# The triangle inverse of the RWKV-7 chunks: left columns only, and the two heads as tiles of 64 rows by 64 columns

## The chip, the cores and the metric

The kernel runs on one core of a Trainium2 chip. The metric is the device time of one execution in microseconds (us), taken as the median of three runs. The profile and the trace are of one further execution of the same program.

## The reference, cut to what matters

The program computes two blocks in a row over 512 tokens (528 in the second, with 16 meta tokens) of width 1024. The change touches only the RWKV-7 layer of the second block. Its recurrence, for each of 32 heads of width 64, is

```python
def step(S, inp):
    r_t, w_t, k_t, v_t, a_t, b_t = inp
    sa = jnp.einsum('bhij,bhj->bhi', S, a_t)
    S = S * w_t[:, :, None, :] + sa[..., None] * b_t[:, :, None, :] + v_t[..., None] * k_t[:, :, None, :]
    return S, jnp.einsum('bhij,bhj->bhi', S, r_t)
```

The kernel does it in chunks of 64 tokens. Inside a chunk the steps hang on each other through a triangular 64x64 matrix, `(I - M)` with `M` strictly triangular, and the kernel needs its inverse for each of the 9 chunks of each head.

## The kernel before

The 32 heads are done as 16 pairs; a tile has head 0 of the pair on partitions 0 to 63 and head 1 on partitions 64 to 127 (`own[0]`, `own[1]`). `all_passes` runs 18 passes, written out for each engine. Pass `i` works on three pairs at once: part A makes the projections of pair `i` (`a_products`, L1348 and L1361), part B the Gram matrices and the inverse of pair `i-1`, part Cs the scan over the chunks of pair `i-2`. Passes 1 to 15 have A and B, pass 16 has B and Cs but no A.

The order on TensorE (PE) is written by hand. First come the nine steps of the scan, each waiting for VectorE (DVE) or ScalarE (ACT); then, in part B, the transposes (L1490), the Gram products (L1499) and the five levels of the inverse. Between the pieces `fill(k)` puts k steps of `a_products`, of four trace records each, or in pass 16 steps of `wo_unit` (L159 to L161 on whole 128x128 weights). `FILL_X` and `FILL_T` put two steps behind each product of a level:

```python
FILL_TURN, FILL_GRAM, FILL_FIRST, FILL_END = 4, 8, 5, 4
FILL_X, FILL_T = (2, 2, 2, 2, 2), (2, 2, 2, 2, 2)
```

The inverse doubles its block size from level to level. `t_m` holds the inverse so far, `t_t` its transpose. A level is: X = M·T (L1510) into PSUM banks 2 and 3; DVE multiplies it with the mask of the level into `x_m` (L1835); the second product with `t_t` (L1526, at level 5 L1528) goes to banks 4 and 5; DVE adds it to `t_m` (L1841) and transposes that (L1844), or at level 5 adds it into `tb` (L1847). The 9 chunks go in two parts of 4 and 5 chunks (`PARTS`), with a semaphore for each.

For each chunk and head there is one call of the matmul with fp32 operands, and each call stands as two records (and two weight loads) in the trace. The contraction runs over all 128 rows: `mb` and `x_m` hold one head and zeros where the other head is, so `mb` is laid out as [128, 9, 128] and `x_m` as [128, 9, 2, 64]. The output of head h has 64 columns of the array. The trace calls such a tile 128*64. `late_pads` writes the zeros once; `x_m` gets its zeros anew from the mask `lv_pad`, which is padded in the same way.

Of the kernel before, what the change touches and what calls it, by code (L numbers as in the profile page):

```python
# [12 lines left out]
ALU = mybir.AluOpType  # L13
# [5 lines left out]
P = 128  # L19
# [51 lines left out]
def program(nc, io, out):  # L71
    with ExitStack() as base:
# [1172 lines left out]
        tb = put("tb", [P, NC_, P])  # L1245
        rb = put("rb", [P, NC_, P])
        t_m = put("t_m", [P, NC_, C])
        x_m = put("x_m", [P, NC_, 2, C])
        t_t = put("t_t", [P, NC_, C])
        bk_rows = put("bk_rows", [P, NC_, P])  # L1250

# [5 lines left out]
        cent, pair_mask = raw[1][:, KD * P:KD * P + P], raw[1][:, KD * P + P:KD * P + P + C]  # L1257
        z_hl = put("z_hl", [P, 2, T2], F32R)
        assert put.end <= LV_PAD, put.end
        lv_pad = region(LV_PAD)("lv_pad", [P, 5, 2, C])  # L1260
        assert LV_PAD + 2.5 <= 147.75

        sb_a, sb_c = xT[:, 0:2, :], xT[:, 2:4, :]
# [43 lines left out]

        def chunks(buf):
            return buf[:].rearrange("p (a b) -> p a b", b=C)

        def halves_of(buf, at=PAD):
            return buf[:, at:at + T2].rearrange("p (a b) -> p a b", a=2)
# [63 lines left out]
        def wo_unit(pe, n):  # L1376

            u = U_WO + n
            pe.wait_ge(split_ready, u + 1)
            if n < 14 or n > 15:  # L1380
                m, half = WO_TILES[n]
                pairs = range(KD * half, (KD if half == 0 else PAIRS - 2 if m < EARLY else PAIRS))
                todo = [(k - KD * half, k, WO_BANKS[m], k == 0, k == (PAIRS - 3 if m < EARLY else PAIRS - 1)) for k in pairs]
                if half == 0:
                    if m == 0:
                        pe.wait_ge(a_ev, 12 * PAIRS)
                        pe.wait_ge(s_z, 48)
                    elif m == 1:
                        pe.wait_ge(wo_ev, 2)
                    elif m == 2:  # L1390
                        pe.wait_ge(tl_ev, 4 * PAIRS)
                        pe.wait_ge(gn_ln, PAIRS - 1)
                    elif m == 4:
                        pe.wait_ge(wo_ev, 4)
                    elif m > 4:
                        pe.wait_ge(m_out, {5: 1, 6: 2, 7: 5}[m])
            else:
                tiles = (0, 1) if n == 14 else (2,)
                pe.wait_ge(wo_ev, 6)
                pe.wait_ge(m_out, 3 if n == 14 else 4)  # L1400
                todo = [(len(tiles) * j + q, PAIRS - 2 + j, LEFT_BANKS[m], j == 0, j == 1) for q, m in enumerate(tiles) for j in range(2)]
            for q, (b, k, banks, start, stop) in enumerate(todo):
                if k >= READY:
                    pe.wait_ge(z_pool, 4 * (k + 1))
                for h in range(2):
                    at = h * (T2 // 2)
                    x = z_hi[:, k, at:at + T2 // 2], z_lo[:, k, at:at + T2 // 2]
                    mm = product(ps[:, banks[h], 0:T2 // 2], block_of(u % 2, b), x, start, stop)
                    if h == 1 and q == len(todo) - 1:
                        mm.then_inc(unit_done, 1)  # L1410
                    yield

        def pass_pe(pe, i, A, B, Cs):
# [17 lines left out]
            for n in range(NC_):  # L1431
                if Cs:
# [11 lines left out]
                    if n == 8:  # L1444
                        pe.wait_ge(yy_ev, 3 * c + 1)
                    if n == 0:
                        pe.wait_ge(tl_ev, 4 * c + 4)
                    for h in range(2):
                        nc.tensor.matmul(y_at(n)[own[h], :], uv[:, n, h, :], rb[:, n, own[h]], start=True, stop=False)
                    if 0 < n < NC_ - 1:  # L1450
# [24 lines left out]
            if B:  # L1475
# [27 lines left out]
                for lv in range(1, 6):  # L1503
                    for p, (c0, m) in enumerate(PARTS):
                        if lv == 1:
                            pe.wait_ge(mb_ev, 4 * b + (2 * p + 2))
                        pe.wait_ge(tm_ev if lv == 1 else tadd_ev, 2 * b + (p + 1) if lv == 1 else 8 * b + (2 * (lv - 2) + p + 1))
                        for x in range(m):
                            for h in range(2):
                                mm = nc.tensor.matmul(ps[own[h], 2 + p, x * C:x * C + C], mb[:, c0 + x, own[h]], t_m[:, c0 + x, :],  # L1510
                                                      start=True, stop=True)
                        mm.then_inc(x_mm, 1)
                        if lv == 1 and p == 0:
                            fill(FILL_FIRST)
                    fill(FILL_X[lv - 1])
                    for p, (c0, m) in enumerate(PARTS):
                        pe.wait_ge(x_ev, 10 * b + (2 * (lv - 1) + p + 1))
                        if lv == 1:
                            pe.wait_ge(t0_ev, 6 * b + (2, 6)[p])
                        else:  # L1520
                            pe.wait_ge(tb_ev, 8 * b + (2 * (lv - 2) + p + 1))
                        for x in range(m):
                            for h in range(2):
                                dst = ps[own[h], 4 + p, x * C:x * C + C]
                                if lv < 5:
                                    mm = nc.tensor.matmul(dst, t_t[:, c0 + x, :], x_m[:, c0 + x, h, :], start=True, stop=True)  # L1526
                                else:
                                    mm = nc.tensor.matmul(dst, x_m[:, c0 + x, h, :], t_t[:, c0 + x, :], start=True, stop=True)  # L1528
                        mm.then_inc(tt_mm, 1)
                    fill(FILL_T[lv - 1])  # L1530
                    if lv == 3 and A:
# [222 lines left out]
            ge(dve, fa, 14 * i + (FA["e_ex"] - 14))  # L1754
            nc.vector.tensor_tensor_scan(lsum[:], restart[:], ws_b[:], 0.0, ALU.mult, ALU.add).then_inc(scanned, 1)

        EARLY_PADS, MIDDLE_PADS, PADS = 6, 14, 20

        def early_pads(dve):
            for h in range(2):  # L1760
# [15 lines left out]
        def late_pads(dve):  # L1776
            dve.wait_ge(mx_done, 4 * KD)
            for buf in (mb, tb, rb):
                nc.vector.memset(buf[:], 0.0).then_inc(pads, 1)
            nc.vector.memset(lv_pad[:], 0.0).then_inc(pads, 1)  # L1780
            dve.wait_ge(pads, PADS - 2)
            for h in range(2):
                nc.vector.tensor_copy(lv_pad[own[h], :, h, :], lv_mask[own[h], 1:6, :]).then_inc(pads, 1)

        def pass_dve(dve, i, A, B, Cs):
            b, c = i - 1, i - 2
# [40 lines left out]
                nc.vector.transpose(t_m[:, c0:c0 + m, :], t_t[:, c0:c0 + m, :]).then_inc(tm_ev, 1)  # L1827

            def part_of(bank, m):
                return ps[:, bank, 0:m * C].rearrange("p (a b) -> p a b", b=C)  # L1830

            def level(lv):
                for p, (c0, m) in enumerate(PARTS):
                    dve.wait_ge(x_mm, 10 * b + (2 * (lv - 1) + p + 1))
                    nc.vector.tensor_tensor(x_m[:, c0:c0 + m, :, :], part_of(2 + p, m).unsqueeze(2).to_broadcast([P, m, 2, C]),  # L1835
                                            lv_pad[:, lv - 1, :, :].unsqueeze(1).to_broadcast([P, m, 2, C]),
                                            ALU.mult).then_inc(x_ev, 1)
                for p, (c0, m) in enumerate(PARTS):
                    dve.wait_ge(tt_mm, 10 * b + (2 * (lv - 1) + p + 1))
                    if lv < 5:  # L1840
                        nc.vector.tensor_tensor(t_m[:, c0:c0 + m, :], part_of(4 + p, m), t_m[:, c0:c0 + m, :],  # L1841
                                                ALU.add).then_inc(tadd_ev, 1)
                        dve.wait_ge(tadd_ev, 8 * b + (2 * (lv - 1) + p + 1))
                        nc.vector.transpose(t_t[:, c0:c0 + m, :], t_m[:, c0:c0 + m, :]).then_inc(tb_ev, 1)  # L1844
                    else:
                        for h in range(2):
                            nc.vector.tensor_tensor(tb[own[h], c0:c0 + m, own[h]], part_of(4 + p, m)[own[h], :, :],  # L1847
                                                    t_t[own[h], c0:c0 + m, :], ALU.add).then_inc(tl_ev, 1)
            if B:
                dve.wait_ge(g_mm, 3 * b + 1)  # L1850
                gram_out(0)
# [28 lines left out]
        def pass_pool(pool, i, A, B, Cs):  # L1880
# [10 lines left out]
            if B:  # L1891

                if Cs:
                    pool.wait_ge(tl_ev, 4 * c + 4)
                held(pool)
                nc.gpsimd.tensor_copy(t_t[:], ident_2[:].unsqueeze(1).to_broadcast([P, NC_, C])).then_inc(eye_done, 1)
                pool.wait_ge(eye_done, b + 1)
# [956 lines left out]
```

## Time and profile before

| | us |
|---|---|
| median of 3 runs | 2376.39 (2374.34 to 2379.22) |
| the profiled execution | 2373.65 |
| span of its trace | 2371.9 |
| PE busy | 2295.2 (97% of the span) |
| DVE busy | 1235.5 (52%) |
| POOL busy | 1142.6 (48%) |
| ACT busy | 851.7 (36%) |

The span is what the trace covers; the profiled execution's own time has 1.75 us around it. "Busy" is time in which at least one instruction of the engine was in flight. PE stands for the matmuls and PEld for the weight loads, which run beside matmuls.

### The profile page before, as it was taken

How to read it: one execution, taken by the hardware profiler on the slowest of the kernel's cores; microseconds unless marked ns; L12 is line 12 of the kernel's file. 1: busy time of each engine (PE TensorE's matmuls, PEld its weight loads, DVE VectorE, ACT ScalarE, POOL GpSimd, SP SyncE). 2: the span in 40 equal slices, each digit the busy share in tenths (PEclk: the TensorE clock that was granted, in tenths of full speed). 3: DMA queues.
4: the chain of work that ended last, by engine and by line, in shares of the span. 5: the costliest groups of instructions: out<-in, count | busy, mean ns of one | idle time of the engine just before them, and what ended most of it. 6: DMA issues, size and time to landing. Idle time of an engine off the chain costs nothing.

```text
span 2371.9 us, 51852 instructions
## 1 busy us (share of the span) xinstructions
PE 2295.2 (97%) x22065; PEld 1789.5 (75%) x22065; DVE 1235.5 (52%) x2284; ACT 851.7 (36%) x1762; POOL 1142.6 (48%) x771
## 2 busy tenths in 40 slices
PE   8999999999999999999999999999899999999898
PEld 7788787788887677777777777777688887777776
DVE  4353278577804555555555555555421566556511
ACT  4122112233302445555555555555221343343300
POOL 4555566866763434443444333344356344344245
PEclk9999999999999999999999999999799999999899
DMA  3333233233322312222222222221523322121212
GB/s 111 89 80 78 83 90 88 80 98 98 108 98 64 92 57 72 69 66 66 66 66 70 72 66 66 66 66 56 183 68 114 105 70 61 41 61 52 83 58 93
DMA packets 263757, 188.07 MB, mean 79 GB/s; under 512 B 18267, under 2 KB 242393, under 8 KB 263145
## 3 DMA queue, kind: packets, MB, share of 16 engines
q1 hardware_dynamic: 263529, 184.76, 26.0%
q8 instruction: 176, 2.88, 0.5%
q14 instruction: 52, 0.43, 0.1%
HBM read 162.69 MB, written 22.04 MB: 78 GB/s over the span
## 4 chain that ended last, share of the span: by engine, by line
PE 61%; DVE 2%; POOL 1%; DMA 1%; issue 1%; ACT 0%; SPq 0%; POOLq 0%; DVEq 0%
PE ps L1348 18%; PE ps L159 7%; PE ps L160 6%; PE ps L161 6%; PE ps L1510 3%; PE ps L1526 3%; PE ps L1552 2%; PE ps L2388 2%; PE ps L1466 1%; PE ps L1499 1%; PE ps L1438 1%; PE ps L1361 1%; PE ps L221 1%; DMA z_lo<-z_kept 1%; PE ps L2374 1%; PE ps L1483 1%
## 5 line engine op out<-in xcount | busy, mean ns | idle before, releaser
L150 POOL TENSOR_TENSOR w_lo<-raw,w_hi 128x1024 fp32r<-128x1024 f32 (+1 forms) x196 | 494.8, 2524 | 16.4
L147 POOL TENSOR_SCALAR w_hi<-raw 128x1024 fp32r<-128x1024 f32 (+1 forms) x196 | 217.1, 1108 | 559.1 <-PE ps L161 542.1
L159 PE MATMUL ps<-h_hi,w_hi 128*128 128x512 f32 x616 | 244.2, 396 | 5.7 <-POOL w_lo L150 4.6
L161 PE MATMUL ps<-h_hi,w_lo 128*128 128x512 f32 x616 | 240.9, 391 | 0.0
L160 PE MATMUL ps<-h_lo,w_hi 128*128 128x512 f32 x616 | 240.4, 390 | 0.0
L1885 POOL TENSOR_TENSOR kp<-k_b,kp 128x528 f32<-128x528 f32 x16 | 29.6, 1847 | 362.0 <-ACT kp L1647 362.0
L1348 PE MATMUL ps<-mixed_r,raw 128*64 128x264 f32 x1024 | 154.4, 391 | 2.3 <-ACT g_b L1589 2.3
L159 PEld LDWEIGHTS ps<-h_hi,w_hi 128*128 128x128 f32 x616 | 116.3, 189 | 31.9 <-POOL w_lo L150 7.2
L1348 PE MATMUL ps<-mixed_k,raw 128*64 128x264 f32 x1024 | 138.3, 389 | 0.0
L161 PEld LDWEIGHTS ps<-h_hi,w_lo 128*128 128x128 f32 x616 | 115.9, 188 | 24.8
L160 PEld LDWEIGHTS ps<-h_lo,w_hi 128*128 128x128 f32 x616 | 116.2, 189 | 23.2
L1835 DVE TENSOR_TENSOR x_m<-ps,lv_pad 128x512 f32<-128x512 f32 (+1 forms) x160 | 115.1, 753 | 33.2 <-PE ps L1510 29.2
L1348 PE MATMUL ps<-mixed_g,raw 128*64 128x264 f32 x1024 | 132.2, 386 | 0.0
L1348 PE MATMUL ps<-mixed_v,raw 128*64 128x264 f32 x1024 | 129.6, 386 | 0.0
L1078 DVE SCALAR_TENSOR_TENSOR up_c<-up_raw,params,up_c 128x512 f32<-128x512 f32 x88 | 111.3, 1266 | 31.8 <-ACT up_c L830 30.2
L1510 PEld LDWEIGHTS ps<-t_m,mb 128*64 128x64 f32 x2880 | 99.9, 138 | 15.0
L1510 PE MATMUL ps<-t_m,mb 128*64 128x64 f32 x2880 | 100.4, 222 | 0.0
L2475 ACT ACTIVATE xT<-ps,nmax 128x144 f32<-128x144 f32 (+1 forms) x64 | 34.6, 541 | 175.2 <-DVE nmax L2498 175.0
L1812 DVE TENSOR_TENSOR gm<-ps,g_mask 128x512 f32<-128x512 f32 (+1 forms) x96 | 47.5, 550 | 91.3 <-PE ps L1499 90.8
L1348 PEld LDWEIGHTS ps<-mixed_v,raw 128*64 128x64 f32 x1024 | 67.2, 137 | 28.6
L1885 POOL TENSOR_TENSOR kk_b<-kk_b,xT 128x528 f32<-128x528 f32 x16 | 21.1, 1318 | 136.6 <-ACT xT L1688 136.5
L1348 PEld LDWEIGHTS ps<-mixed_g,raw 128*64 128x64 f32 x1024 | 66.0, 137 | 26.2
(447 smaller groups left out, 5862.1 us busy)
## 6 DMA issues: line engine op xcount, KB each, us to landing
raw<-in_rwkv_w_in_dram SPq DMA_DIRECT2D x64, 512.0 KB, 4.0
raw<-in_w_up_dram SPq DMA_DIRECT2D x44, 512.0 KB, 3.9
raw<-in_w_in_dram SPq DMA_DIRECT2D x41, 512.0 KB, 3.8
raw<-in_w_down_dram SPq DMA_DIRECT2D x22, 512.0 KB, 3.5
raw<-in_mla_w_in_dram SPq DMA_DIRECT2D x22, 512.0 KB, 4.0
sb_kept<-xT SPq DMA_DIRECT2D x16, 528.0 KB, 3.0
xT<-sb_kept SPq DMA_DIRECT2D x16, 528.0 KB, 4.2
raw<-in_rwkv_w_out_dram SPq DMA_DIRECT2D x16, 512.0 KB, 4.5
```

Of the source, the lines that this page charges most:

```text
L147: nc.gpsimd.tensor_scalar(w_hi[s][:, 0:width], raw[s][:, 0:width], 1.0, 0.0, ALU.mult, ALU.add).then_inc(split_hi, 1)
L150: nc.gpsimd.tensor_tensor(w_lo[s][:, 0:width], raw[s][:, 0:width], w_hi[s][:, 0:width].bitcast(F32), ALU.subtract).then_inc(split_ready, 1)
L159: nc.tensor.matmul(dst, w[0], x[0], start=start, stop=False)
L160: nc.tensor.matmul(dst, w[0], x[1], start=False, stop=False)
L161: return nc.tensor.matmul(dst, w[1], x[0], start=False, stop=stop)
L1078: nc.vector.scalar_tensor_tensor(out=up_c[:, ab, 1 + k, :], in0=up_raw[:, n % 4, 1 - k:1 - k + T1], scalar=prm(("cf1", "cf0")[k], n // 2 + ...
L1348: mm = nc.tensor.matmul(dst[m, :], raw_k[t % 2][:, k, m], mixed[t][:, k, cols], start=(k == 0), stop=(k == KD - 1))
L1510: mm = nc.tensor.matmul(ps[own[h], 2 + p, x * C:x * C + C], mb[:, c0 + x, own[h]], t_m[:, c0 + x, :], start=True, stop=True)
L1526: mm = nc.tensor.matmul(dst, t_t[:, c0 + x, :], x_m[:, c0 + x, h, :], start=True, stop=True)
L1812: nc.vector.tensor_tensor(gm[:, c0:c0 + m, :, own[h]], gram_of(q, h).rearrange("p a (k c) -> p a k c", k=2), g_mask[:].rearrange("p (k c) ...
L1835: nc.vector.tensor_tensor(x_m[:, c0:c0 + m, :, :], part_of(2 + p, m).unsqueeze(2).to_broadcast([P, m, 2, C]), lv_pad[:, lv - 1, :, :].unsq ...
L1885: nc.gpsimd.tensor_tensor(dst, x, y, op).then_inc(pa, 1)
```

## The change

Of a level's product only the left columns of each pair of blocks can change, 32 of 64. The new kernel takes only these as the moving operand (`left`), packs them side by side in PSUM (`packed`), and takes for each head only its own 64 partitions, for weights and moving operand. So each matmul of L1510, L1526 and L1528 becomes one of 64 rows, 64 weight columns and 32 moving columns. `x_m` and `lv_pad` lose the room for the other head. At level 5 the lower left block alone is computed; DVE first copies all of `t_t` into `tb` and then writes that block over it, so `tl_ev` counts 6 a pair instead of 4. The two lines of waits on `tl_ev` follow. `mb`, `tb` and `rb` stay padded, since the scan uses them.

```diff
-        x_m = put("x_m", [P, NC_, 2, C])
+        H = C // 2
+        x_m = put("x_m", [P, NC_, C])
...
-        lv_pad = region(LV_PAD)("lv_pad", [P, 5, 2, C])
+        lv_pad = region(LV_PAD)("lv_pad", [P, 5, H])
...
+        def left(ap, lv):
+            s = 1 << lv
+            if len(ap.shape) == 2:
+                return ap.rearrange("p (a t s) -> p a t s", t=2, s=s)[:, :, 0, :]
+            return ap.rearrange("p m (a t s) -> p m a t s", t=2, s=s)[:, :, :, 0, :]
...
                         for x in range(m):
                             for h in range(2):
-                                mm = nc.tensor.matmul(ps[own[h], 2 + p, x * C:x * C + C], mb[:, c0 + x, own[h]], t_m[:, c0 + x, :],
-                                                      start=True, stop=True)
+                                mm = nc.tensor.matmul(packed(ps[own[h], 2 + p, x * H:x * H + H], lv), mb[own[h], c0 + x, own[h]],
+                                                      left(t_m[own[h], c0 + x, :], lv), start=True, stop=True)
...
-                                dst = ps[own[h], 4 + p, x * C:x * C + C]
+                                dst = ps[own[h], 4 + p, x * H:x * H + H]
                                 if lv < 5:
-                                    mm = nc.tensor.matmul(dst, t_t[:, c0 + x, :], x_m[:, c0 + x, h, :], start=True, stop=True)
+                                    mm = nc.tensor.matmul(dst, t_t[own[h], c0 + x, :], x_m[own[h], c0 + x, 0:H], start=True, stop=True)
                                 else:
-                                    mm = nc.tensor.matmul(dst, x_m[:, c0 + x, h, :], t_t[:, c0 + x, :], start=True, stop=True)
+                                    mm = nc.tensor.matmul(dst, x_m[own[h], c0 + x, :], t_t[own[h], c0 + x, H:C], start=True, stop=True)
...
-            nc.vector.memset(lv_pad[:], 0.0).then_inc(pads, 1)
-            dve.wait_ge(pads, PADS - 2)
-            for h in range(2):
-                nc.vector.tensor_copy(lv_pad[own[h], :, h, :], lv_mask[own[h], 1:6, :]).then_inc(pads, 1)
+            nc.vector.memset(x_m[:, :, H:C], 0.0).then_inc(pads, 1)
+            for lv in range(1, 6):
+                nc.vector.tensor_copy(packed(lv_pad[:, lv - 1, :], lv), left(lv_mask[:, lv, :], lv)).then_inc(pads, 1)
...
-                    nc.vector.tensor_tensor(x_m[:, c0:c0 + m, :, :], part_of(2 + p, m).unsqueeze(2).to_broadcast([P, m, 2, C]),
-                                            lv_pad[:, lv - 1, :, :].unsqueeze(1).to_broadcast([P, m, 2, C]),
-                                            ALU.mult).then_inc(x_ev, 1)
+                    nc.vector.tensor_tensor(x_m[:, c0:c0 + m, 0:H], part_of(2 + p, m),
+                                            lv_pad[:, lv - 1, :].unsqueeze(1).to_broadcast([P, m, H]), ALU.mult).then_inc(x_ev, 1)
+                if lv == 5:
+                    dve.wait_ge(tb_ev, 8 * b + 8)
+                    for h in range(2):
+                        nc.vector.tensor_copy(tb[own[h], :, own[h]], t_t[own[h], :, :]).then_inc(tl_ev, 1)
+                    dve.wait_ge(tl_ev, 6 * b + 2)
...
-                        nc.vector.tensor_tensor(t_m[:, c0:c0 + m, :], part_of(4 + p, m), t_m[:, c0:c0 + m, :],
-                                                ALU.add).then_inc(tadd_ev, 1)
+                        grown = left(t_m[:, c0:c0 + m, :], lv)
+                        nc.vector.tensor_tensor(grown, packed(part_of(4 + p, m), lv), grown, ALU.add).then_inc(tadd_ev, 1)
...
                         for h in range(2):
-                            nc.vector.tensor_tensor(tb[own[h], c0:c0 + m, own[h]], part_of(4 + p, m)[own[h], :, :],
-                                                    t_t[own[h], c0:c0 + m, :], ALU.add).then_inc(tl_ev, 1)
+                            nc.vector.tensor_copy(tb[C * h:C * h + H, c0:c0 + m, C * h + H:C * h + C],
+                                                  part_of(4 + p, m)[C * h:C * h + H, :, :]).then_inc(tl_ev, 1)
```

On PE the order stays and the number of instructions too. This is the end of part B of a pass with A before the change, levels 4 and 5 (the sizes are output partitions by moving columns, `mixed_g` marks the fills):

```order
L1552 MATMUL ps<-sq_b,halves_ones 64x264 x4
L1510 MATMUL ps<-t_m,mb 64x64 x18
L1348 MATMUL ps<-mixed_g,raw 64x264 x4
L1526 MATMUL ps<-x_m,t_t 64x64 x18
L1348 MATMUL ps<-mixed_g,raw 64x264 x4
L1510 MATMUL ps<-t_m,mb 64x64 x18
L1348 MATMUL ps<-mixed_g,raw 64x264 x4
L1528 MATMUL ps<-t_t,x_m 64x64 x18
L1348 MATMUL ps<-mixed_g,raw 64x264 x4
```

And this is the same place with the change:

```order
L1565 MATMUL ps<-sq_b,halves_ones 64x264 x4
L1523 MATMUL ps<-t_m,mb 64x32 x18
L1361 MATMUL ps<-mixed_g,raw 64x264 x4
L1539 MATMUL ps<-x_m,t_t 64x32 x18
L1361 MATMUL ps<-mixed_g,raw 64x264 x4
L1523 MATMUL ps<-t_m,mb 64x32 x18
L1361 MATMUL ps<-mixed_g,raw 64x264 x4
L1541 MATMUL ps<-t_t,x_m 64x32 x18
L1361 MATMUL ps<-mixed_g,raw 64x264 x4
```

Nothing moved there; the stretches of the inverse stand where they stood, with half the moving columns, and the fills between them are the same tiles as before. On DVE this is level 5 before the change:

```order
L1835 TENSOR_TENSOR x_m<-ps,lv_pad 128x512
L1835 TENSOR_TENSOR x_m<-ps,lv_pad 128x640
L1847 TENSOR_TENSOR tb<-ps,t_t 64x4x64 x2
L1847 TENSOR_TENSOR tb<-ps,t_t 64x5x64 x2
L1878 TENSOR_TENSOR xT<-y_c,xT 128x528
```

And level 5 with the change:

```order
L1847 TENSOR_TENSOR x_m<-ps,lv_pad 128x4x32
L1847 TENSOR_TENSOR x_m<-ps,lv_pad 128x5x32
L1852 COPY tb<-t_t 64x9x64 x2
L1863 COPY tb<-ps 32x4x32 x2
L1863 COPY tb<-ps 32x5x32 x2
L1894 TENSOR_TENSOR xT<-y_c,xT 128x528
```

Two copies of 64x576 come in between the mask and the last product's results, and the four instructions behind them are small.

## Rows read from the trace of the kernel before

**Rows 1.** The page: busy times, and the chain that ended last.
```profile
PE 2295.2 (97%) x22065; PEld 1789.5 (75%) x22065; DVE 1235.5 (52%) x2284; ACT 851.7 (36%) x1762; POOL 1142.6 (48%) x771
...
PE 61%; DVE 2%; POOL 1%; DMA 1%; issue 1%; ACT 0%; SPq 0%; POOLq 0%; DVEq 0%
PE ps L1348 18%; PE ps L159 7%; PE ps L160 6%; PE ps L161 6%; PE ps L1510 3%; PE ps L1526 3%; PE ps L1552 2%; PE ps L2388 2%; PE ps L1466 1%; PE ps L1499 1%; PE ps L1438 1%; PE ps L1361 1%; PE ps L221 1%; DMA z_lo<-z_kept 1%; PE ps L2374 1%; PE ps L1483 1%
```

**Rows 2.** Stretches of one pass: scan, part B, Gram products.
```profile
core 0: us, PE busy (x) PEld busy (x) DVE busy (x) ACT busy (x) POOL busy (x), PEclk, DMA share, GB/s
1203.18:1224.54 21.36, 21.02 (x316) 12.63 (x313) 7.62 (x29) 8.55 (x27) 10.33 (x9) 1.00 0.40 130
1224.54:1260.65 36.11, 36.11 (x629) 28.10 (x631) 24.94 (x49) 21.28 (x41) 13.02 (x10) 1.00 0.11 31
1228.76:1230.97 2.21, 2.21 (x39) 2.09 (x37) 1.00 (x2) 1.75 (x4) 0.00 (x0) 1.00 0.00 0
```

**Rows 3.** Chain through level 2 of that pass: start us, us, what.
```profile
1240.85 1.05 PE ps L1510 x36
1241.90 0.89 PE ps L1348 x8
1242.79 1.05 PE ps L1526 x36
```

**Rows 4.** Groups, whole span: busy us, mean ns, then idle before them.
```profile
L1835 DVE TENSOR_TENSOR x_m<-ps,lv_pad 128x512 f32<-128x512 f32 (+1 forms) x160 | 115.1, 753 | 33.2 <-PE ps L1510 29.2
L1510 PEld LDWEIGHTS ps<-t_m,mb 128*64 128x64 f32 x2880 | 99.9, 138 | 15.0
L1499 PEld LDWEIGHTS ps<-rkv,bk 64*128 64x128 f32 x576 | 33.4, 188 | 6.2 <-issue 6.2
```

**Rows 5.** Timeline of PE: matmuls with 16 moving columns.
```profile
47.65 1.95 PE L623 MATMUL ps<-x_diag,meta_rows 16*128 16x16 f32 x16
49.45 0.33 PE L628 MATMUL ps<-ident,meta_rows 16*128 16x16 f32 x3
```

**Rows 6.** Timeline of PE in that pass, around the Gram products.
```profile
1226.83 2.00 PE L1348 MATMUL ps<-mixed_k,raw 128*64 128x264 f32 x16
1228.76 2.28 PE L1499 MATMUL ps<-rkv,bk 64*128 64x128 f32 x36
1230.97 2.45 PE L1348 MATMUL ps<-mixed_k,raw 128*64 128x264 f32 x20
...
1237.27 0.75 PE L1510 MATMUL ps<-t_m,mb 128*64 128x64 f32 x20
1237.85 1.06 PE L1348 MATMUL ps<-mixed_v,raw 128*64 128x264 f32 x8
```

**Rows 7.** Timeline of PE in pass 16, fills on 128*128 tiles.
```profile
1710.99 0.28 PE L160 MATMUL ps<-z_lo,w_hi 128*128 128x264 f32 x1
1711.11 0.28 PE L161 MATMUL ps<-z_hi,w_lo 128*128 128x264 f32 x1
1711.33 1.27 PE L1526 MATMUL ps<-x_m,t_t 128*64 128x64 f32 x36
1712.53 0.39 PE L159 MATMUL ps<-z_hi,w_hi 128*128 128x264 f32 x1
1712.76 0.28 PE L160 MATMUL ps<-z_lo,w_hi 128*128 128x264 f32 x1
```

**Rows 8.** Timeline of DVE at level 5 of a pass with fills.
```profile
1256.72 1.92 DVE L1847 TENSOR_TENSOR tb<-ps,t_t 64x256 f32<-64x256 f32 x4 [0.52 <-PE ps L1528]
```

**Rows 9.** Timeline of PE at level 5 of pass 16, without fills.
```profile
1722.47 1.53 PE L1528 MATMUL ps<-t_t,x_m 128*64 128x64 f32 x36 [0.21 <-DVE x_m L1835]
...
1725.18 0.34 PE L1449 MATMUL ps<-rb,uv 128*64 128x64 f32 x4 [1.05 <-DVE tb L1847]
```

**Rows 10.** Copies on DVE, for their durations (min/median/max in the second).
```profile
L1790 DVE COPY p_sb<-ps 128x64 f32<-128x64 f32 x90 | 20.2, 224 | 48.1 <-PE ps L1438 48.1
L1783 DVE COPY lv_pad<-lv_mask x2: 479/480/482, 804.1 to 804.6; 64x320 f32<-64x320 f32 x2
```

More of the change, by code:

```diff
@@ L1309, in chunks, with packed @@
             return buf[:].rearrange("p (a b) -> p a b", b=C)
+        def left(ap, lv):
[3 more added lines that the diff above has]
+            return ap.rearrange("p m (a t s) -> p m a t s", t=2, s=s)[:, :, :, 0, :]
+        def packed(ap, lv):
+            s = 1 << lv
+            if len(ap.shape) == 2:
+                return ap.rearrange("p (a s) -> p a s", s=s)
+            return ap.rearrange("p m (a s) -> p m a s", s=s)
         def halves_of(buf, at=PAD):
@@ L1390, in wo_unit @@
                     elif m == 2:
-                        pe.wait_ge(tl_ev, 4 * PAIRS)
+                        pe.wait_ge(tl_ev, 6 * PAIRS)
                         pe.wait_ge(gn_ln, PAIRS - 1)
@@ L1446, in pass_pe @@
                     if n == 0:
-                        pe.wait_ge(tl_ev, 4 * c + 4)
+                        pe.wait_ge(tl_ev, 6 * c + 6)
                     for h in range(2):
@@ L1755, in decay_scan @@
             nc.vector.tensor_tensor_scan(lsum[:], restart[:], ws_b[:], 0.0, ALU.mult, ALU.add).then_inc(scanned, 1)
-        EARLY_PADS, MIDDLE_PADS, PADS = 6, 14, 20
+        EARLY_PADS, MIDDLE_PADS, PADS = 6, 14, 23
         def early_pads(dve):
@@ L1829, in part_of @@
             def part_of(bank, m):
-                return ps[:, bank, 0:m * C].rearrange("p (a b) -> p a b", b=C)
+                return ps[:, bank, 0:m * H].rearrange("p (a b) -> p a b", b=H)
             def level(lv):
@@ L1893, in pass_pool @@
                 if Cs:
-                    pool.wait_ge(tl_ev, 4 * c + 4)
+                    pool.wait_ge(tl_ev, 6 * c + 6)
                 held(pool)
```

## The prediction

> **What bounds the kernel now.** I began with the page. TensorE is busy for 97% of the span and the chain that ended last lies on it; the three lines of the inverse are in that chain, L1348 (the projections) leads it [rows 1]. Shares say little about a stage, so I next cut out one pass with all three parts. Its scan takes 21.36 us, of which TensorE is busy for 21.02; part B takes 36.11 us, and TensorE is busy for all of it [rows 2]. So in part B no wait on DVE or ScalarE is left to remove: what TensorE's own queue takes there is the time, and the 0.34 us of idleness in the scan belong to a round trip that the change doesn't touch. DVE, at 24.94 us of 36.11, is no bound [rows 2].
>
> The third view is the chain inside part B. A product of all nine chunks is 36 records in 1.05 us, and the two steps of fill behind it are 8 records in 0.89 us [rows 3]. The reader is to see that they alternate with nothing in between. There are ten products a pass. Since the first product of level 1 is split by a fill, they stand in 11 stretches, with other work before and behind each.
>
> **What a matmul of the inverse costs.** Records run two at a time, one for each head's tile: 20 records of L1510 take from 1237.27 to 1237.85 [rows 6], so 0.058 us a pair. A record streams 64 columns in two passes (0.89 us for 4 pairs of 264 columns is 0.223 us a pair [rows 3], 0.84 ns a column), which is 0.054 us. It also loads 64 weight columns. The record of a load of 64 columns lasts 138 ns and of 128 columns 188 ns [rows 4]: 50 ns for 64 columns. So both explain 0.058, and the question of this case is which of them binds once the stream is halved. The change halves the moving columns and leaves the number of loads and the weight columns of each.
>
> The row that tells them apart is at the start of the kernel: 16 matmuls with 16 moving columns, 16 rows and 128 weight columns take from 47.65 to 49.45 [rows 5], 0.1125 us each. Their stream is 16 x 0.84 = 13 ns. What is left is the load, at some 0.11 us for 128 columns, whatever the rows. Half of that is 0.056 us for 64 columns, and two tiles load side by side as they do now. So I take 0.058 us a pair after the change too: the stretch of 36 records stays at 1.05 us, and the gain of half a stream is nothing. The bounds: 0.053 us a pair at best (the load with no gap), 0.09 us less a product of 18 pairs; a pair whose stream is all that counts is a rival below.
>
> **What the new tile costs.** The products now are tiles of 64 rows and 64 columns between fills of 128 rows and 64 columns. The trace shows what it costs to go from one shape to another. From L1348 to the Gram products, which have 64 rows and 128 columns: 16 records of L1348 start at 1226.83 and the Gram products at 1228.76 [rows 6], so 1.93 us where 8 pairs of 0.223 are 1.78, and 0.05 of the rest is the fill's first load, itself behind such a change. 0.10 us is left, and the loads, which otherwise run ahead, sat idle for it (6.2 us in 16 passes before L1499 [rows 4]). Pass 16 shows a stretch of the inverse itself among fills of another shape. Before it, 0.22 us go from 1711.11 to 1711.33 where the records of that fill are otherwise 0.12 apart (1710.99 to 1711.11): **0.10 us** to get in. The stretch then takes from 1711.33 to 1712.53, 1.20 us [rows 7] against 1.05 [rows 3]: 0.15, which I split as **0.05** for the first load, no longer hidden, and **0.10** to get out. The fill's first record takes 0.23 (1712.53 to 1712.76 [rows 7]) for 0.12, and its weights have 128 columns; the fills of passes 1 to 15 have 64, so **0.05**. Sum 0.30 us a stretch.
>
> The Trainium skill says that "Changing tiling mode (not just tile) drains the TensorE" (TensorEngine Tiling (Array Packing), Key Properties). It gives no size, and the trace agrees with it at 0.10 us each way; by the rule alone, the stretches would pay 22 times a pass. [...]
>
> Stretches that pay: 11 in each of passes 1 to 15, 165 in all. In pass 16 the fills are 128*128 and the price is paid already. 165 x 0.30 = **+49.5 us**. Bounds: only the two drains (0.20) gives 33; the whole of pass 16's price, 128 columns of weights reloaded (0.36), gives 59.
>
> **DVE.** The mask product falls from 753 ns [rows 4] to about 0.3 us for 128 or 160 elements (my estimate, between 224 ns for 64 elements [rows 10] and 753 for 576), the sum to some 0.3 us. It is off the path in passes 1 to 15, hidden by the fills; were the fills gone it would count, and in pass 16 they are. There the mask product held up the second product by 0.21 us at level 5 and the scan waited 1.05 us for `tb` [rows 9]; level 4 looks the same. With the mask 0.8 us shorter both waits of 0.2 go. Behind it the two new copies of 64x576 (0.48 us for 320 elements [rows 10], so about 0.75 each) and four small ones (about 0.2 each, by the 224 ns of 64 elements) are 2.3 us, against 1.92 now [rows 8]. So `tb` is ready 0.4 us earlier. **-1 us**, between -3 and +1. In the other passes the copies run while TensorE has fills and the head sums (3.56 us, 32 records at 0.89 us for 8) before the scan asks for `tb`.
>
> **Pads.** One memset and two copies of 0.48 us [rows 10] become a smaller memset and five copies of about 0.2 us, once: nothing, within 0.5 us.
>
> **Sum.** 2373.65 + 49.5 - 1 = 2422.2 for the profiled execution. It lay 2.7 us below the median of the runs, so I forecast **2425 us** for the median, 2.0% slower.
>
> **The rivals.**
> - *No price between the shapes.* It could be that 128*64 and 64*64 count as one shape, since the columns are alike; the trace has only changes of columns, and of rows and columns together. Then nothing but the 1 us is left: 2375 us, no change. Against it: the loads alone don't need 0.10 us at L1499, and getting out of the one row shape and getting into the other cost the same.
> - *The stream binds.* A pair would cost 27 + 5 ns = 0.032 us, a product 0.47 us less; ten products in 16 passes are -75 us. With the price of the shapes 2425 - 75 = 2350 us, faster by 1.1%; without it 2300. It decides once a pair takes less than 0.041 us (49 us over 160 x 18 pairs are 0.017). The 0.1125 us of [rows 5] speak against it.
> - *Load and stream in a row.* If a tile of 64 rows can't load while it streams, a pair costs 0.058 + 0.027, a product 0.49 us more: +78, so 2503 us. The 16 matmuls of [rows 5] show overlap on 16 rows, so this is unlikely.
> - The clock might fall, since two tiles of 64 by 64 are half of the array. In the Gram products, with 64 rows in each tile, it was granted in full (1.00 [rows 2]).
>
> **How the numbers follow.** The price without gain 0.80, one shape 0.08, the stream binds 0.08 (both forms), more than that 0.04. Range of the likeliest: with 33 us and the best pair (160 x 0.09 = 14 less) 2395; the dear end, 59 us and +1 for pass 16, 2437. The first needs two bounds at once, so I take 2400 to 2438, which leaves out about 2 in 10. What a measurement of this kernel can tell from no change is about 0.2% (5 us). Faster 0.09, same 0.08, slower 0.83.
>
> **What would show it.** In the profile after: a product of 36 records among fills takes 1.15 to 1.25 us from its start to the fill's, a fill of 8 records some 1.0 from its start to the next product's; part B of a pass with fills is 39.4 us for 36.11, and the scan is still 21.4. The loads of the new tiles still last about 138 ns. The mask product is near 0.3 us and DVE's busy time lower by some 70 us, with nothing gained by it. I am wrong if the fill of 8 records keeps its 0.89 us (no price), or if 36 records take 0.6 us (the stream binds).

## The result and the profile after

The changed kernel took 2418.11 us in the median of four runs (2414.83 to 2421.35), the kernel before in the same session 2375.36 (2373.66 to 2379.22). The ratio is 1.018 with a 95% interval of 1.0164 to 1.0195: 43 us slower. The forecast was 2425.

The page of the kernel after, its busy times and the head of its chain:

```profile
span 2416.5 us, 51903 instructions
...
PE 2339.6 (97%) x22065; PEld 1788.7 (74%) x22065; DVE 1164.0 (48%) x2319; ACT 849.1 (35%) x1762; POOL 1141.0 (47%) x771
...
PE 61%; DVE 2%; POOL 1%; DMA 1%; issue 1%; ACT 0%; SPq 0%; POOLq 0%; DVEq 0%
```

Against [rows 1] TensorE is busy for 44.4 us more and the span is 44.6 us longer, while DVE is busy for 71.5 us less. All of the loss is TensorE's own time. The windows of one pass, its scan and its part B (us, then busy time and instructions of each engine, clock, DMA share, GB/s):

```profile
1224.25:1245.61 21.36, 21.02 (x316) 12.56 (x313) 7.62 (x29) 8.36 (x27) 9.79 (x9) 1.00 0.41 130
1245.61:1284.68 39.07, 39.07 (x630) 27.99 (x631) 20.43 (x51) 21.33 (x41) 13.49 (x10) 1.00 0.10 29
```

The scan takes what it took in [rows 2]. Part B is 2.96 us longer than the 36.11 us of [rows 2], with TensorE busy for all of it and as many instructions (one record more at the edge of the window). The clock is granted in full in both. The chain through level 2 of this pass (start us, us, what), beside [rows 3]:

```profile
1262.73 1.17 PE ps L1523 x36
1263.90 1.04 PE ps L1361 x8
1264.94 1.17 PE ps L1539 x36
```

A product went from 1.05 to 1.17 us although it streams half the columns, and the fill, which the change doesn't touch, from 0.89 to 1.04. The first number holds the way out of the tiles and the second the way in. Together that is 0.27 us a stretch (from one run of the tiles to the next), and 165 of these are 44.6 us.

The instructions of L1523 (min/median/max in ns) and what TensorE's loads waited for:

```profile
L1523 PEld LDWEIGHTS ps<-t_m,mb x2880: 128/135/136, 833.6 to 1766.1; 64*64 64x64 f32 x192
L1523 PE MATMUL ps<-t_m,mb x2880: 218/220/241, 833.6 to 1766.1; 64*64 64x32 f32 x192
...
  issue: 36.2, 91
```

The load of one tile has hardly changed (138 ns in [rows 4]). "issue: 36.2, 91" means that 91 times, 36.2 us in all, the loads stood idle before such a stretch and nothing that the profile shows held them. With the short ones the idle time before this line's loads is 36.9 us, where it was 15.0 us [rows 4]. In the trace of the kernel before, the first load of a product starts 0.22 us ahead of its matmul; in the changed kernel it starts 0.002 us ahead. So loads run ahead of the matmuls there, but not across a change of shape.

### The profile page after: what moved, and what is told of

Same layout as the page of the kernel before. It is cut to its first block, busy times and chain, and to the rows that moved or that the text cites. A ratio compares the mean times of both kernels' runs of the same rounds, so it can differ in the third digit from the quotient of the medians.

```text
span 2416.5 us, 51903 instructions
## 1 busy us (share of the span) xinstructions
PE 2339.6 (97%) x22065; PEld 1788.7 (74%) x22065; DVE 1164.0 (48%) x2319; ACT 849.1 (35%) x1762; POOL 1141.0 (47%) x771
## 4 chain that ended last, share of the span: by engine, by line
PE 61%; DVE 2%; POOL 1%; DMA 1%; issue 1%; ACT 0%; SPq 0%; POOLq 0%; DVEq 0%
PE ps L1361 18%; PE ps L159 7%; PE ps L160 6%; PE ps L161 6%; PE ps L1523 4%; PE ps L1539 3%; PE ps L1565 2%; PE ps L2404 2%; PE ps L1512 1%; PE ps L1479 1%; PE ps L1451 1%; PE ps L1374 1%; PE ps L221 1%; DMA z_lo<-z_kept 1%; PE ps L2390 1%; PE ps L1496 1%
## 5 line engine op out<-in xcount | busy, mean ns | idle before, releaser
L1523 PEld LDWEIGHTS ps<-t_m,mb 64*64 64x64 f32 x2880 | 91.5, 135 | 36.9 <-issue 36.2
L1523 PE MATMUL ps<-t_m,mb 64*64 64x32 f32 x2880 | 102.1, 221 | 0.0
L1847 DVE TENSOR_TENSOR x_m<-ps,lv_pad 128x128 f32<-128x128 f32 (+1 forms) x160 | 49.1, 307 | 90.6 <-PE ps L1523 90.1
L1539 PEld LDWEIGHTS ps<-x_m,t_t 64*64 64x64 f32 x2304 | 72.3, 135 | 24.4 <-issue 23.9
```

What stands on the lines that cost most here:

```text
L1523: mm = nc.tensor.matmul(packed(ps[own[h], 2 + p, x * H:x * H + H], lv), mb[own[h], c0 + x, own[h]], left(t_m[own[h], c0 + x, :], lv), star ...
L1539: mm = nc.tensor.matmul(dst, t_t[own[h], c0 + x, :], x_m[own[h], c0 + x, 0:H], start=True, stop=True)
L1847: nc.vector.tensor_tensor(x_m[:, c0:c0 + m, 0:H], part_of(2 + p, m), lv_pad[:, lv - 1, :].unsqueeze(1).to_broadcast([P, m, H]), ALU.mult). ...
```

## The experiments

The kernel before ran beside each of them; the ratios are to it.

**The left columns alone, on the old tiles.** `x_m` and `lv_pad` get their room for the other head back, and all 128 rows are contracted:

```diff
-                                    mm = nc.tensor.matmul(dst, t_t[own[h], c0 + x, :], x_m[own[h], c0 + x, 0:H], start=True, stop=True)
+                                    mm = nc.tensor.matmul(dst, t_t[:, c0 + x, :], x_m[:, c0 + x, h, 0:H], start=True, stop=True)
```

> One half of the change alone: the left columns only (32 moving columns for 64), but on the old tiles of 128 rows and 64 columns with the zeros for the other head. My theory (the load of 64 weight columns sets the pace, and the change of tile shape is the price): a product of 36 records stays at 1.05 us and a fill at 0.89 us, so 2370 to 2376 us, the few us only from pass 16, where DVE is waited for. The rival (the stream sets the pace): a product takes about 0.57 us and the kernel some 2300 us. If the price of the changed kernel comes from the short strided columns and not from the tiles, this one pays it too: 2418 us.

It took 2380.44 us against 2374.65, ratio 1.0019 (1.0009 to 1.0029), 4 us above what I expected. The passes are those of before, 57.47 us each; the chain shows the same sum of product and fill as [rows 3], 1.94 us:

```profile
1256.29 1.02 PE ps L1539 x36
1257.31 0.92 PE ps L1361 x8
```

Most of the loss is ahead of the passes: the first record of the scan comes 4.8 us later in the trace. The padded mask needs ten small copies in this kernel, and they stand on DVE's queue ahead of the sum for which the first head sums wait. The groups of DVE, and TensorE's waits (us, times, longest):

```profile
L1798 DVE COPY lv_pad<-lv_mask 64x32 f32<-64x32 f32 x10 | 4.1, 412 | 0.3
PE ps L1565 <- DVE xT L1891: 6.0, 1, 6.0
```

In the kernel before this wait is 1.7 us. To be sure, the copies went behind that sum, with a wait for them at the start of the next pass:

```diff
+        def level_pads(dve):
...
+                if i == 1:
+                    dve.wait_ge(pads, ALL_PADS)
...
+                if i == 0:
+                    level_pads(dve)
```

> The left columns on the old tiles again, with the writing of the masks and pads of the levels moved behind DVE's first sum of squares (L1891 there), where DVE has 14 us to spare. The first version kept the passes at their length, but DVE wrote masks for 5.9 us before that instruction and TensorE waited 6.02 us for it instead of 1.74. My theory (the 32 columns themselves give and cost nothing): that wait falls below 1 us and the kernel comes to 2370 to 2376 us. If the columns had a cost of their own it would stay near 2380.

2374.57 us against 2376.42, ratio 1.0002 (0.9991 to 1.0012), as expected; the wait is 0.9 us. So half the moving columns on 128*64 tiles are worth nothing, in the total as in each stretch. The end of pass 16 is not free in either version: from the last product of the inverse to the last record of the scan it takes some 36.4 us for 32.9, and shorter parts behind the passes make up for some of it.

**The tiles alone, with all 64 moving columns.** Taken as a diff to the kernel before:

```diff
-                                mm = nc.tensor.matmul(ps[own[h], 2 + p, x * C:x * C + C], mb[:, c0 + x, own[h]], t_m[:, c0 + x, :],
+                                mm = nc.tensor.matmul(ps[own[h], 2 + p, x * C:x * C + C], mb[own[h], c0 + x, own[h]], t_m[own[h], c0 + x, :],
                                                       start=True, stop=True)
...
-                                    mm = nc.tensor.matmul(dst, t_t[:, c0 + x, :], x_m[:, c0 + x, h, :], start=True, stop=True)
+                                    mm = nc.tensor.matmul(dst, t_t[own[h], c0 + x, :], x_m[own[h], c0 + x, :], start=True, stop=True)
```

> The other half alone: tiles of 64 rows and 64 columns, all 64 moving columns. My theory: 0.10 us to get in, 0.05 for the first load, 0.10 to get out and 0.05 for the fill's first load, so a product of 1.20 us, a fill of 1.04 us, 165 stretches, 2420 to 2426 us, and some 4 us above the changed kernel, whose product took 1.17. The rival (no price between the shapes; the changed kernel pays for its short columns): 1.05 and 0.89 us, 2375 us.

2420.68 us against 2374.65, ratio 1.0196 (1.0182 to 1.021). The whole loss is in the tiles. Its chain:

```profile
1262.12 1.20 PE ps L1526 x36
1263.31 1.04 PE ps L1348 x8
```

The product is at 1.20 us here, 0.03 above the 1.17 of 32 columns, and the fill is equal. So on these tiles half the stream does give a little, 27 ns a stretch, the stream of 32 columns. The loads show it at the way out: the first load of the fill starts 0.203 us behind the last load of the product with 64 moving columns and 0.176 us with 32. The matmuls show the same time at the start of the product. There 0.107 us lie between the starts of the first and the second pair with 64 columns and 0.080 with 32, while the way out is 0.15 us in both. The longest records of this kernel's product, 267 ns for the 241 of L1523 above, are those first pairs (min/median/max in ns):

```profile
L1526 PE MATMUL ps<-x_m,t_t x2304: 218/218/267, 837.5 to 1769.3; 64*64 64x64 f32 x192
```

**Fewer stretches.** Both fills of a level behind the second product:

```diff
-        FILL_X, FILL_T = (2, 2, 2, 2, 2), (2, 2, 2, 2, 2)
+        FILL_X, FILL_T = (0, 0, 0, 0, 0), (4, 4, 4, 4, 4)
```

> The changed kernel with the two steps of fill between the two products of a level moved behind the second (FILL_X 0, FILL_T 4), so that 6 stretches a pass stand where 11 stood. My theory (the price is paid at each change of shape, 0.27 us a stretch): 75 stretches less are 20 us, and the mask of DVE now stands uncovered between the products, 0.1 to 0.3 us a level, which gives back 7 to 22 us: 2398 to 2420 us, likeliest 2406. The rival (the price lies inside the products, or per record): the products cost what they cost and the waits come on top, 2425 to 2440 us.

2408.0 us, ratio 1.0142 (1.0129 to 1.0155), 10 us less than the changed kernel, as expected: five stretches a pass fewer had promised 20, and a wait for the mask was to take part of it back. The two products of a level, now side by side, take 1.17 and 1.20 us. The first record of the second comes 0.18 us behind the last of the first, where pairs are otherwise 0.05 apart, so 0.13 us of it is the wait, which with the slow first pair behind it is 0.15 us a level. Five levels give 5 x (0.27 - 0.15) = 0.60 us, and a pass takes 59.83 us for the 60.43 of the changed kernel. The number of matmuls is the same in both, so the price hangs on the number of changes.

**Eight moving columns.** In both products; the mask is zero and the sum adds 0 times the product, so the inverse's results are left out:

```diff
-                                    mm = nc.tensor.matmul(dst, t_t[own[h], c0 + x, :], x_m[own[h], c0 + x, 0:H], start=True, stop=True)
+                                    mm = nc.tensor.matmul(dst, t_t[own[h], c0 + x, :], x_m[own[h], c0 + x, 0:8], start=True, stop=True)
```

> The changed kernel with 8 moving columns in each product of the inverse instead of 32; weights as before, 64 columns. The results of the inverse are left out (masks zero, sums without the product), so that it stays at its first blocks. My theory (the load binds): product and fill stay at 1.15 to 1.17 and 1.04 us, 2415 to 2418 us. The rival (part of the pace is stream): 24 columns less are 20 ns a pair or 0.36 us a product, 58 us in all, 2360 us.

In one run, 2487.93 us against 2373.69. As a total this is far off what either theory expected; in the stretches the load's theory is right. The chain and the windows show both (in the windows the number behind the busy times is the clock):

```profile
1247.48 1.15 PE ps L1523 x36
1248.63 1.89 PE ps L1361 x8
1250.52 2.02 PE ps L1539 x36
...
1257.10 1.04 PE ps L1361 x8
1258.14 1.15 PE ps L1539 x36
```
```profile
1249.50:1255.50 6.00, 6.00 (x56) 3.87 (x54) 1.57 (x4) 0.00 (x0) 0.00 (x0) 0.50 0.23 69
1257.00:1263.00 6.00, 6.00 (x106) 4.29 (x106) 2.65 (x8) 2.12 (x4) 0.36 (x1) 1.00 0.01 3
```

At the full clock a product is 1.15 us with a quarter of the columns, only 0.02 less than with 32: the stream doesn't bind. The loads show these 0.02 at the way out again, 0.156 us for 0.176.
**Half the weight columns.** 32 weight columns and 32 moving ones; here too the inverse's results are left out.

```diff
-                                mm = nc.tensor.matmul(packed(ps[own[h], 2 + p, x * H:x * H + H], lv), mb[own[h], c0 + x, own[h]],
+                                mm = nc.tensor.matmul(packed(ps[C * h:C * h + H, 2 + p, x * H:x * H + H], lv), mb[own[h], c0 + x, C * h:C * h + H],
                                                       left(t_m[own[h], c0 + x, :], lv), start=True, stop=True)
```

> The changed kernel with 32 weight columns instead of 64 and 32 moving columns, so that each product gives only the upper half of its output columns; the results of the inverse are left out as in the run with 8 columns. It makes tiles of 64 rows and 32 columns. My theory (the load binds): a pair falls from 0.058 to about 0.032 us, the product to some 0.65 us, 160 x 0.5 = 80 us less, 2338 us, with the fill at 1.04 as before. The rival (a fixed time per record binds): the product stays near 1.15 and the kernel at 2415 us.

In one run, 2337.81 us, and the mean granted clock is 0.991:

```profile
1226.33 0.69 PE ps L1523 x36
1227.02 1.04 PE ps L1361 x8
```

A product of 0.69 us for 1.17, with as many instructions and moving columns. What a pair takes is the load of its weight columns. The Trainium skill says that the time of a load goes by its columns and not by the contraction rows (TensorE: Matmul & The Clock Gate, LDWEIGHTS (loading the stationary operand)). The trace agrees, with (1.17 - 0.69) / 18 = 27 ns for 32 columns here, and with 0.058 us a pair for 128 rows as for 64.

**All four tiles.** The changed kernel uses two tiles on the diagonal of four. Here the odd chunks of a part go to the other two; the inverse's results are left out.

```diff
-                                dst = ps[own[h], 4 + p, x * H:x * H + H]
+                                dst = ps[own[h ^ (x & 1)], 4 + p - 2 * (x & 1), x * H:x * H + H]
```

> The changed kernel with the odd chunks on the two tiles that lie idle (head 0 into output partitions 64 to 127, head 1 into 0 to 63, in a bank of their own), from the second level on. The results of the inverse are not used here: the masks are zero and the sums leave the product out, so the inverse stays at its first blocks; the instructions and their sizes are the same. If four tiles can load side by side, two chunks take what one takes now and a product falls from 1.17 to about 0.65 us, 16 passes with 9 products, near 2345 us. If the array takes two loads at a time, whatever the tiles, it stays at 1.17 and 2418 us. I hold the two for equally likely.

In one run, 2350.84 us. The chain at levels 1 and 2 (the first product of level 1 is still on two tiles):

```profile
1228.60 1.04 PE ps L1361 x8
1229.64 0.70 PE ps L1539 x36
1230.34 1.04 PE ps L1361 x8
1231.38 0.70 PE ps L1523 x36
```

Four tiles load side by side: a group of four records takes the 0.058 us that a pair takes on two tiles, and 36 records take 0.70 us.

**Four tiles in earnest.** From level 2 on the odd chunks have their product in the other head's half, so `t_t` and `x_m` keep them there, and DVE transposes them across (`turn`), three instructions a part for one:

```diff
-                        nc.vector.transpose(t_t[:, c0:c0 + m, :], t_m[:, c0:c0 + m, :]).then_inc(tb_ev, 1)
+                        turn(p)
...
+            def turn(p):
+                c0, m = PARTS[p]
+                nc.vector.transpose(t_t[:, c0:c0 + m:2, :], t_m[:, c0:c0 + m:2, :]).then_inc(tb_ev, 1)
+                for h in range(2):
+                    nc.vector.transpose(t_t[own[1 - h], c0 + 1:c0 + 4:2, :], t_m[own[h], c0 + 1:c0 + 4:2, :]).then_inc(tb_ev, 1)
```

> The whole inverse on four tiles, from level 2 on: the odd chunks are held in the transpose with the heads' halves swapped, so that the first product of an odd chunk goes from rows of head h to the other 64 columns and the second comes back. DVE pays with three transposes in place of one (even chunks on 128 partitions, odd chunks in two of 64). From the run with four tiles: a product takes 0.70 us instead of 1.17, so 8 products in 16 passes are 60 us less than the changed kernel, 2358 us. DVE then works some 3.0 us in a level of 3.5; if a hidden wait between transposes and the next product appears instead, each level costs up to 0.5 us more, 30 us in all, 2388 us, no better than before.

2418.03 us, ratio 1.0177 (1.0159 to 1.0196): a miss by 60 us. The chain of one pass shows where TensorE lost what its products had gained:

```profile
1271.30 0.70 PE ps L1527 x36
1272.00 1.04 PE ps L1361 x8
...
1276.30 0.56 DVE x_m L1872 x2
1277.14 0.73 DVE tb L1879
...
1278.59 1.42 DVE tb L1878
1280.04 1.41 DVE tb L1879
...
1282.86 1.95 DVE xT L1928
```

The four copies into `tb` and the sum behind them are DVE's, and the scan waits for them. It takes 24.4 us a pass for 21.3. DVE, which the 2358 us took to be hidden, was the bound. The clock adds to it: behind these waits it is at 0.50 for 3.4 us in nine of the fourteen passes that have all three parts, and their scans are 24.2 to 24.8 us, where four of the other five, at the full clock, take 23.6. The same kernel with the fills of a level behind its second product:

> The same with the fill between the two products of a level moved behind the second (FILL_X 0, FILL_T 4). In the changed kernel this gave 10 us where the changes of shape alone were worth 20: the rest went to the mask. Now a product is shorter, so the mask is covered less: X of the second part covers 0.39 us of the 0.5 that the mask of the first needs. I expect 5 us less to 5 us more than the version that isn't joined, near 2356 us.

2382.78 us, ratio 1.0026 (1.0012 to 1.0039). This is a miss as well, by 27 us, and the step from the version before it is 35 us and not the 5 that I gave it: the scan is back at 21.4 us in the median. The levels are a chain on DVE:

```profile
1253.31 0.30 DVE t_m L1889
1253.64 0.31 DVE t_t L1860
1253.98 0.31 DVE t_t L1862
1254.32 0.31 DVE t_t L1862
1254.66 0.37 DVE t_m L1889
```

A transpose of 64x128 costs 0.31 us, that of 128x256, four times the elements, is 0.45 us in the changed kernel. It is the small pieces that make DVE late.

Two steps against this: the copies into `tb` go to ScalarE, behind its `logs()`, and then three transposes a level for all nine chunks.

```diff
+            if B:
+                act.wait_ge(tb_ev, 24 * b + 24)
+                for h in range(2):
+                    nc.scalar.activation(tb[own[h], 0:NC_:2, own[h]], t_t[own[h], 0:NC_:2, :], ACT.Copy).then_inc(tl_ev, 1)
+                    nc.scalar.activation(tb[own[h], 1:NC_:2, own[h]], t_t[own[1 - h], 1:NC_:2, :], ACT.Copy).then_inc(tl_ev, 1)
```

> The joined version on four tiles, with the copies of the transpose into the scan's operand (four, 2.9 us a pass, at level 5 ahead of the last results) on ScalarE instead of DVE, and the masks written off the path. In the joined version DVE bound the end of a pass: its copies, the last results and its product for the group norm held up the scan. My theory: TensorE is fed again there, the pass is 2 to 2.9 us shorter and the kernel 30 to 45 us, so 2340 to 2353 us, and for the first time less than the kernel before. The rival (ScalarE is late with its own items, or level by level the transposes bind anyway): less than 15 us, 2368 us or more.

> The same with the three transposes of a level done once for all nine chunks instead of once for each part: 3 instead of 6, some 1.3 instead of 1.97 us of DVE a level, in 4 levels of 16 passes. In the joined version DVE took 3.67 us a level and had no gap, TensorE some 3.5. My theory: 0.1 us a level, 64 levels, 6 to 8 us less than the run with the copies on ScalarE. If the first part's transpose is what the second product waits for, it comes later now and this is slower than that run.

2389.91 us, ratio 1.0052 (1.0036 to 1.0067), and 2387.41, ratio 1.0051 (1.0034 to 1.0069). Both are misses for one reason, and the second step, of which I expected 6 to 8 us, gave nothing that these intervals can tell. The timeline of ScalarE in the first:

```profile
1265.87 0.70 ACT L1703 ACTIVATE xT<-ps,eps_col 128x528 f32<-128x528 f32 x1 [3.37 <-PE ps L1571]
...
1267.65 1.28 ACT L1712 ACT_TABLE_LOAD   x1
1268.94 0.47 ACT L1763 ACTIVATE tb<-t_t 64x320 f32<-64x320 f32 x1
```

ScalarE waits 3.37 us for the last head sums, does its logarithms, loads a table and only then copies. The copies had been put behind work that ends last in the pass, and the scan, at 22.5 us for 21.3, waited for them.

**The best version.** The last kernel, with the copies ahead of the logarithms and the fills of the changed kernel:

```diff
-        FILL_X, FILL_T = (0, 0, 0, 0, 0), (4, 4, 4, 4, 4)
+        FILL_X, FILL_T = (2, 2, 2, 2, 2), (2, 2, 2, 2, 2)
...
-            logs()
             if B:
                 act.wait_ge(tb_ev, 12 * b + 12)
...
+            logs()
```

> The version with the transposes at once, with two edits: ScalarE copies the transpose into the scan's operand before the logarithms of the pass instead of behind them (there DVE waited 3.9 us a pass for those copies and TensorE 0.8 us for DVE), and the fill stands between the products again (2 and 2), since with 3 transposes a level DVE needs 2.0 us from the end of a product to its last transpose, and two fills and the next product now cover 1.7 us of it and more. My theory: TensorE binds again, a pass is 56.3 to 56.8 us for 57.47 before the change, 15 passes, 10 to 18 us less than the kernel before: 2357 to 2365 us. The rival (DVE or ScalarE late once more at the start of the scan): a pass of 58 us and more, 2380 us.

2367.5 us against 2376.13, ratio 0.9961 (0.9949 to 0.9974). It beats both kernels, by less than I expected. A pass is 56.73 us for 57.47, and the scan is back at 21.34. From the first record of the scan to the last product of the inverse the trace gains 9.8 us. Pass 16 gives 5.8 us of it back, between that product and the last record of the scan. The windows there, before and in the fall of the clock, and timelines of TensorE and DVE:

```profile
1710.00:1714.00 4.00, 3.35 (x116) 2.53 (x116) 2.84 (x8) 1.19 (x3) 0.00 (x0) 1.00 0.00 0
1715.80:1725.90 10.10, 8.39 (x51) 7.17 (x52) 2.36 (x8) 2.83 (x6) 5.89 (x6) 0.50 0.08 11
```
```profile
1715.38 0.34 PE L1453 MATMUL ps<-uv,gm 128*64 128x64 f32 x4 [1.47 <-DVE tb L1899]
```
```profile
1714.63 1.36 DVE L1899 COPY tb<-ps 32x128 f32<-32x128 f32 x4 [1.32 <-ACT tb L1763]
1717.32 0.71 DVE L1934 TENSOR_TENSOR xT<-y_c,xT 128x528 f32<-128x528 f32 x1 [1.33 <-ACT xT L1710]
```

Without fills of `a_products` the copies and the transposes across the halves are on the path, TensorE waits, and the clock then falls to 0.50 for some 10 us, so the waits are, by this reading, paid a second time. That the fall follows from the waits was not tried by itself. Around the start of pass 16, too, the clock is at 0.50 for longer than in the kernel before (34 us for 24); why was not looked into.

## Why the prediction was right, and where it was off

**The load binds (right).** I said that a pair takes 0.058 us before and after, since the load of 64 weight columns takes it, and that [rows 5] tells load and stream apart. A quarter of the moving columns takes 0.02 us off a product, half the weight columns 0.48. The rival in which the stream binds (product 0.6 us) is dead, and so is that of load and stream in a row.

**Half a stream is worth nothing (nearly).** This is the step with the miss in size. I put the product at 1.20 us with 32 columns; it is 1.17, and 1.20 is what it takes with 64. Of the four terms of the 0.30 us, three came as forecast. The fourth, 0.05 for the product's first load that is no longer hidden, was taken from a stretch with 64 moving columns; with 32 the first pair takes 0.080 us for 0.056, so 0.024. A pair's stream is hidden by the next pair's load, but at a change of shape there is none beside it, and the stream of one pair counts. The loads bear this out at the way out: 0.203, 0.176 and 0.156 us with 64, 32 and 8 columns are steps of 27 and 20 ns, which are 32 and 24 columns at 0.84 ns. So half a stream is worth 0.027 us once in each stretch. 165 stretches make 4.5 us of it, and 49.5 becomes 44.6 with what the rounded terms leave.

**The price between the shapes (right).** 0.10 us in, 0.10 us out, and the fill's own first load 0.05 (0.274 us from its first pair to its second, for 0.225). Start to start, the first record of a product now comes 0.316 us behind the last one of the fill where it was 0.216, and the first record of the fill 0.150 us behind the last of the product where it was 0.052. The fill of 8 records is at 1.04 for the "some 1.0" of the forecast. The 6.2 us of idle loads that I named at L1499 are 0.39 us a pass and not a measure of the 0.10: the loads stop ahead of the matmuls. That 128*64 and 64*64 might be one shape was the rival of no change, and the kernel with the tiles alone denies it. The Trainium skill says that changing tiling mode "drains the TensorE" (TensorEngine Tiling (Array Packing), Key Properties), and these rows agree with it. Its "Up to 2×" for a small dimension of at most 64 (Theoretical Speedup) is not seen when the rows go from 128 to 64 on two tiles: 1.17 us for 1.05. With four tiles it is 0.70, 1.5 times as fast as before, which agrees with what the Key Properties say of different tiles, that they can load weights and multiply in parallel.

**The passes (right).** Part B takes 39.07 us for the 39.4 forecast, less by the 0.03 us of each of 11 stretches. The scan is unchanged at 21.32 in the median of the passes, and DVE's busy time fell by 71.5 us with nothing gained. The mask product is at 0.29 to 0.32 us.

**Pass 16 (wrong in sign, within its bounds).** I forecast `tb` 0.4 us earlier and -1 us. The timelines of DVE and TensorE at level 5:

```profile
1766.65 1.51 DVE L1852 COPY tb<-t_t 64x576 f32<-64x576 f32 x2
1768.19 1.29 DVE L1863 COPY tb<-ps 32x128 f32<-32x128 f32 x4
```
```profile
1769.54 0.42 PE L1462 MATMUL ps<-rb,uv 128*64 128x64 f32 x4 [1.73 <-DVE tb L1863]
```

The copies take 2.80 us in place of 2.3, since the four small ones are at 0.29 to 0.32 each and not at the 0.2 that I took from a copy of 64 elements. The scan waits 1.73 us for 1.05 [rows 9], and in the 3 us behind it the clock is granted at 0.50. From the first record of the scan to the last product of the inverse the trace is 40.3 us longer, where 14 passes of 2.96 more are 41.4, so the levels of pass 16 gave 1.1 us; from there to the last record of the scan it is 2.1 us longer. That is +1.0.

**Pads (right for this kernel).** The five copies are 1.8 us, not 1.0, of which the path saw 0.2 us (a wait of 1.9 for 1.7). The first experiment showed how near that was: with ten copies it was 4 us.

**The sum.** 2373.65 + 44.6 + 1.0 is 2419.2, and the profiled execution took 2418.2; the rest lies in the parts outside the passes. The last 2.7 us of my 2425 came from three runs of the kernel before, all of them slower than its profiled execution; over all 65 of its runs here its median is 2375.6, 0.7 us lower. The changed kernel's profiled execution is at its median, so these 2.7 us were a term without a counterpart.

## What to carry to other kernels

A tile smaller than the array saves nothing by itself: while the load of the weight columns binds, as in this kernel, fewer moving columns and fewer rows save next to nothing. What counts is how many stretches of another shape stand between other work (0.27 us each here) and whether all tiles that load side by side are in use. And the engine that is idle for half the time can be the next bound, once its work is cut into many small instructions and the last of them is what the next stage waits for.

## What the runs showed of the hardware that I had not expected

Four 64*64 tiles load side by side: 36 records in 0.70 us where two tiles take 1.17. With eight moving columns on two such tiles the granted clock fell to its lower level inside passes in which TensorE was busy throughout, for some 230 us of the span in the one run, and not with 32 columns (60 us); what it was about the eight columns was not taken apart. In pass 16 the wait of TensorE for `tb` was followed by 3 to 7 us at 0.50 where it was 1.72 to 1.84 us (the changed kernel, the one with fewer stretches, and the left columns with the pads off the path). It was not where it was 1.05 or 0.99 us (the kernel before, and the tiles alone). In the last kernel waits of 1.01, 0.53 and 1.47 us in a row were followed by 10 us. At a change of shape the loads, which otherwise start 0.22 us ahead of their matmuls, start with them. On DVE an instruction of 32 or 64 partitions and 128 elements is hardly cheaper (0.29 to 0.31 us) than one of 128 partitions (0.29).
